# A two-layer conditioned trunk on eight cores: the planner's vector durations and load rate are set to measured values

## The chip, the cores and the metric

The kernel runs on the 8 cores of one Trainium2 chip. Each core takes one of the 8 batch rows and computes it alone, so every core runs the same program on other data. The metric is the device time of the slowest core in microseconds (us), the median of several runs; lower is better. A core has a matrix engine (TensorE, in the rows PE, its weight loads PEld), a vector engine (VectorE, DVE), an activation engine (ScalarE, ACT), a general engine (GpSimd, POOL) and an engine that here only issues transfers (SyncE, SP). Each engine works through its own list of instructions in order, and semaphores tie the lists together.

## What is computed

Batch 8, 4096 positions, width 1024, two layers. Layer 0 mixes positions by a short gated convolution and a gated recurrence, layer 1 by spatial gating; each is followed by a squared-ReLU MLP. Cut to what matters:

```python
for layer in range(2):
    sh1, sc1, g1, sh2, sc2, g2 = ada_modulation(c, ada_w[layer], ada_b[layer])
    h = rmsnorm(x, norm_mix_g[layer]) * (1.0 + sc1) + sh1
    if layer == 0:
        p = einsum('bsd,de->bse', h, w_in0)          # 1024 -> 3584
        y = concat([short_conv_mixer(...), hgrn2_mixer(...)]) @ w_out0
    else:
        z = gelu(einsum('bsd,de->bse', h, w_in1) + b_in1)   # 1024 -> 2048
        y = spatial_gating_mixer(z, ...) @ w_out1
    x = x + g1 * y
    h = rmsnorm(x, norm_ffn_g[layer]) * (1.0 + sc2) + sh2
    hid = square(relu(h @ w_ff1[layer]))             # 1024 -> 4096
    x = x + g2 * (hid @ w_ff2[layer])                # 4096 -> 1024
return rmsnorm(x, final_g)
```

## The kernel before

A core's 4096 positions are 8 tiles of 512. The work goes through six stages, one after the other, each over all 8 tiles: the mixer of layer 0 (phase_m0, 82 to 641 us of the profiled execution), its MLP in two passes (p 0: 562 to 1059, p 1: 1043 to 1462), the mixer of layer 1 (phase_m1, 1438 to 1831), and its MLP in two passes (1803 to 2252, 2237 to 2653). x lies in HBM between the stages; each pass of an MLP holds half of the hidden width, 8 weight slots of 2 MiB, and the slots are refilled as the last tile of the stage before gives them up (L582: 2 MiB of float32 in HBM, which land as 1 MiB of bfloat16). Every stage begins a tile with a norm: squares of the 8 chunks of x on ScalarE (L693 and L696), their sum on GpSimd (L699), one product on TensorE (L701), then L703 and L705 on ScalarE.

A pass with p 0 is ff1 (product groups of 8 matmuls at L750, evicted by ScalarE at L1207 and squared at L1210 or, on VectorE, at L1213) and ff2_plain (L1328, added to x by VectorE at L1340). A pass with p 1 computes its products with 7 instead of 8 half-size products: ff1_halves and ff2. In ff1_halves a tile has 8 columns m, and each goes through three groups of 8 matmuls of 256 columns (0.87 us each) in one PSUM bank, all of them recorded at L1233, with a fourth, shared by two columns:

- first(m): ScalarE copies half of the bank out (L1247), VectorE adds the other half (L1248);
- shared(i): VectorE subtracts it from the two parts (L1269);
- second(m): it writes over the half that L1247 and L1248 have read, so it waits for both; ScalarE evicts it (L1260) and squares it (L1254);
- third(m): it writes over what L1260 has read, so it waits for that; VectorE adds the part (L1278), and ReLU and square follow (L1282 on VectorE for some columns, else L1286 and L1254 on ScalarE).

ff2 does the same with four columns (products at L1371, copies at L1394 and L1396, the shared product's at L1407, additions to x at L1378). Its last part is stage(m, (7, 6)) for m 0 to 3.

No instruction's place is written by hand. Each call of pe, act, dve or dma records an operation with its reads and writes, a key (when it is wanted, in us) and a duration. Graph.schedule then plays the program through with these durations: whenever an engine is free, it takes the available operation with the lowest key, and that becomes the engine's order. A duration is a number for ordering alone; nothing on the chip is delayed by it. VectorE's come from c_dve or stand as numbers; a transfer's is its bytes by a rate:

```python
def c_dve(n, rate=1, ptr=0):
    return 0.155 + n / (960.0 * rate) + 0.06 * ptr
```

With H = 256 and TT = 512, c_dve(H) is 0.422 us, c_dve(TT) 0.688 us, c_dve(H, 1, 1) 0.482 us. What the chip does between two instructions is kept by semaphores whatever the order, so a bad order shows as an engine that waits with its first instruction while a later one is ready.

## Time and profile before

| | us |
|---|---|
| median of 3 runs | 2675.32 (2668.88 to 2678.11) |
| the profiled execution | 2666.36 |
| its span on the slowest core (core 3) | 2664.8 |
| spans of the eight cores | 2655.8 to 2664.8 |
| TensorE, VectorE, ScalarE, GpSimd busy | 2563.7, 1872.8, 1486.2, 853.9 |

The profiled execution is 9.0 us (0.3%) below the median of the runs shown. The views below are of core 3. In a view of the time line each row is a run of instructions of one line: start, length, engine, line, operation, output and input, their number, and in brackets the idle time before it and what ended it. Neighbouring matmuls overlap in the records, so their lengths are compared by the distance of their starts.

### The profile page before, as it was taken

To read this page: it belongs to the slowest core of one execution; us is meant where nothing else is said; L and a number is where in the kernel's file an instruction comes from. 1 tells how busy PE (TensorE), PEld (TensorE's weight loads), DVE (VectorE), ACT (ScalarE), POOL (GpSimd) and SP (SyncE) were. 2 spreads that over 40 slices of the span, in tenths; PEclk is the share of its full clock that TensorE was granted. 3 is DMA by queue.
4 is the path that set the end of the run, shared out by engine and by line. 5 is a ranking of instruction groups with operands and counts; after the bars stand their busy time and mean duration, and the time that the engine had idled before them with its cause. 6 is when DMAs were issued, how large, how long until landed. Compare 5 with 4: busy or idle time off the path is not lost.

```text
span 2664.8 us, 53173 instructions; the slowest of 8 cores (2655.8 to 2664.8 us)
## 1 busy us (share of the span) xinstructions
PE 2563.7 (96%) x18204; PEld 1684.9 (63%) x18204; DVE 1872.8 (70%) x3391; ACT 1486.2 (56%) x2477; POOL 853.9 (32%) x952
## 2 busy tenths in 40 slices
PE   3999999999999999999999999998999999999998
PEld 1444454445666666788887444444766666788887
DVE  3577777777655666887887677776655656787887
ACT  4777777784545553343434676644545553545544
POOL 4555555542533440000002354412434440112111
PEclk9999999999999999999999999999999999999999
DMA  9844444449366348754538666553254336332431
GB/s 191 149 139 112 112 112 109 103 98 199 89 148 147 101 120 149 179 132 131 146 108 171 179 180 190 146 156 110 87 144 134 96 116 152 92 118 80 134 106 64
DMA packets 126426, 348.34 MB, mean 131 GB/s; under 512 B 13904, under 2 KB 16464, under 8 KB 115280
## 3 DMA queue, kind: packets, MB, share of 16 engines
q1 hardware_dynamic: 106464, 265.77, 32.9%
q0 software_dynamic: 19152, 78.65, 18.1%
q8 instruction: 149, 2.44, 0.4%
q14 instruction: 117, 0.96, 0.1%
q10 hardware_dynamic: 544, 0.52, 0.1%
HBM read 301.90 MB, written 117.44 MB: 157 GB/s over the span
## 4 chain that ended last, share of the span: by engine, by line
PE 79%; DMA 7%; POOL 4%; issue 3%; ACT 3%; DVE 3%; SPq 0%; DVEq 0%; ACTq 0%; POOLq 0%
PE ps L750 25%; PE ps L1328 14%; PE ps L1371 14%; PE ps L1233 10%; PE ps L1639 4%; PE ps L1584 3%; PE ps L1018 3%; POOL sb_arena L699 2%; DMA sb_arena<-xs 2%; PE ps L1193 2%; DMA xs<-sb_arena 2%; PE ps L991 2%; DMA sb_arena<-w_in 1%; DMA sb_arena<-x 1%; DMA sb_arena<-w_ff 1%
## 5 line engine op out<-in xcount | busy, mean ns | idle before, releaser
L750 PE MATMUL ps<-sb_arena 128*128 128x512 bf16 x4096 | 923.0, 381 | 6.5 <-DMA sb_arena<-w_in 6.5
L750 PEld LDWEIGHTS ps<-sb_arena 128*128 128x128 bf16 x4096 | 396.2, 98 | 463.8 <-issue 13.7
L699 POOL TENSOR_TENSOR sb_arena<-sb_arena 128x512 f32<-128x512 f32 (+1 forms) x259 | 357.1, 1379 | 795.9 <-ACT sb_arena L696 772.0
L1328 PE MATMUL ps<-sb_arena 128*128 128x256 bf16 x3584 | 402.9, 274 | 5.4 <-DVE sb_arena L1213 5.3
L1371 PE MATMUL ps<-sb_arena 128*128 128x256 bf16 x3584 | 398.6, 273 | 4.7 <-DVE sb_arena L1378 4.7
L1328 PEld LDWEIGHTS ps<-sb_arena 128*128 128x128 bf16 x3584 | 351.7, 98 | 57.3 <-issue 8.1
L1371 PEld LDWEIGHTS ps<-sb_arena 128*128 128x128 bf16 x3584 | 350.4, 98 | 46.8 <-issue 5.7
L1233 PE MATMUL ps<-sb_arena 128*128 128x256 bf16 x3136 | 351.9, 272 | 2.1 <-DVE sb_arena L1248 1.6
L1207 ACT ACTIVATE sb_arena<-ps 128x512 f32<-128x512 f32 x288 | 170.7, 594 | 292.8 <-PE ps L750 211.3
L1233 PEld LDWEIGHTS ps<-sb_arena 128*128 128x128 bf16 x3136 | 304.9, 98 | 43.3 <-issue 8.0
L1340 DVE SCALAR_TENSOR_TENSOR sb_arena<-ps,sb_arena 128x256 f32<-128x256 f32 x640 | 261.1, 474 | 87.3 <-PE ps L1328 86.2
L1311 DVE TENSOR_TENSOR sb_arena<-sb_arena 128x1024 bf16<-128x1024 bf16 x320 | 249.4, 815 | 65.6 <-ACT sb_arena L1210 57.4
L696 ACT ACTIVATE sb_arena<-sb_arena 128x512 f32<-128x512 f32 x273 | 169.1, 624 | 104.3 <-POOL sb_arena L699 40.8
L1213 DVE TENSOR_TENSOR sb_arena<-sb_arena 128x512 bf16<-128x512 f32 x90 | 77.9, 865 | 170.7 <-ACT sb_arena L1207 170.7
L412 ACT ACT_TABLE_LOAD x128 | 164.2, 1283 | 57.6 <-PE ps L750 30.1
L1176 POOL TENSOR_TENSOR sb_arena<-sb_arena 128x512 f32<-128x512 f32 x112 | 138.4, 1275 | 99.0 <-ACT sb_arena L705 98.8
L1179 ACT ACTIVATE sb_arena<-sb_arena 128x512 bf16<-128x512 f32 x128 | 103.8, 813 | 72.7 <-POOL sb_arena L1176 61.9
L1378 DVE SCALAR_TENSOR_TENSOR sb_arena<-ps,sb_arena 128x256 f32<-128x256 f32 x256 | 110.5, 477 | 41.5 <-PE ps L1371 38.4
L1210 ACT ACTIVATE sb_arena<-sb_arena 128x512 bf16<-128x512 f32 x198 | 124.4, 628 | 15.1
L1639 PE MATMUL ps<-sb_arena 128*128 128x512 bf16 x512 | 121.6, 384 | 9.4 <-DVE sb_arena L1632 7.1
L740 DVE SCALAR_TENSOR_TENSOR sb_arena<-ps,sb_arena 128x512 f32<-128x512 f32 x128 | 94.3, 740 | 42.6 <-PE ps L1018 26.8
L1584 PE MATMUL ps<-sb_arena 128*128 128x512 bf16 x512 | 121.7, 382 | 1.8 <-ACT sb_arena L727 1.8
(152 smaller groups left out, 3066.8 us busy)
## 6 DMA issues: line engine op xcount, KB each, us to landing
xs<-sb_arena SPq DMA_DIRECT2D x320, 256.0 KB, 4.5
sb_arena<-xs SPq DMA_DIRECT2D x160, 512.0 KB, 6.5
sb_arena<-w_ff POOLq DMA_DIRECT2D x32, 1024.0 KB, 12.9
sb_arena<-ada_w POOLq DMA_DIRECT2D x72, 256.0 KB, 4.9
sb_arena<-x SPq DMA_DIRECT2D x64, 256.0 KB, 3.9
hs<-sb_arena SPq DMA_DIRECT2D x16, 1024.0 KB, 12.8
sb_arena<-hs SPq DMA_DIRECT2D x16, 1024.0 KB, 5.2
sb_arena<-xs SPq DMA_DIRECT2D x64, 256.0 KB, 4.6
```

Source lines behind the costliest of these rows:

```text
L412: eng.preload_act_table_set(op.table)
L696: act(lambda e, c=c, ap=ap: e.activation(out=tmp[:, c % 2, :], in_=ap, func=AF.Square), b, [tmpb[c % 2]], key, c_act(512))
L699: G.add(adds, lambda e, c=c, to=to: e.tensor_tensor(out=to, in0=dst, in1=tmp[:, c % 2, :], op=ALU.add), [b_dst, tmpb[c % 2]], [b_to], key, ...
L750: parts = [(lambda e, kc=kc: e.matmul(bk(B), w[:, kc, col0:col0 + 128], hT[:, kc, :], start=kc == 0, stop=kc == 7), [wb, hb[kc]], c_mm(512 ...
L1207: act(lambda e, B=B, q=q: e.activation(out=rt[:, q, :], in_=bk(B), func=AF.Relu), [B], rtb[2 * q:2 * q + 2], k, c_act(TT, True))
L1233: parts.append((lambda e, kc=kc, r=r, w=w: e.matmul(bk(B)[:, col:col + H], w[:, kc, (m % 4) * 128:(m % 4) * 128 + 128], r[:, kc, :], start ...
L1311: dve(lambda e, xa=xa, ya=ya, da=da, op=op: e.tensor_tensor(out=da, in0=xa, in1=ya, op=op), xbufs + ybufs, dbufs, k + (8.0 if u == 0 else ...
L1328: parts.append((lambda e, m=m, fc=fc, h=h, r=r: e.matmul(bk(Bm)[:, h * H:(h + 1) * H], w[:, fc, m * 128:(m + 1) * 128], r, start=h == 0 an ...
L1340: dve(lambda e, h=h, x=x, g=g: e.scalar_tensor_tensor(out=x, in0=bk(Bm)[:, h * H:(h + 1) * H], scalar=g, in1=x, op0=ALU.mult, op1=ALU.add) ...
L1371: parts.append((lambda e, fc=fc, r=r: e.matmul(bk(B)[:, col:col + H], w[:, fc, m * 128:(m + 1) * 128], r, start=start and fc == 0, stop=fc ...
L1584: o = pe([(lambda e, kc=kc, g=g, hh=hh, B=B, hT=hT: e.matmul(bk(B), hT[:, kc, g * 128:(g + 1) * 128], win[2 + hh][0][:, kc, :], start=kc == 0,
L1639: pe([(lambda e, kk=kk, c=c, B=B, wv=wv: e.matmul(bk(B), wv[:, kk, (c % 4) * 128:(c % 4) * 128 + 128], ymix[:, kk, :], start=kk == 0, stop ...
```

## The change

Six numbers that VectorE operations are recorded with, and the rate of transfers. No operation is added, removed or given another key; what changes is the play through, and with it the order on each engine.

```diff
@@ Graph.schedule
-                        t = pick.nbytes / 280e3
+                        t = pick.nbytes / 320e3
@@ first (L1248), shared (L1269), ff2's first (L1396) and shared_product (L1407)
-                        0.34)
+                        c_dve(H))
@@ third (L1278)
-                        [B, tb], [zb], k - 20, 0.62)
+                        [B, tb], [zb], k - 20, c_dve(TT))
@@ ff2's add (L1378)
-                        0.38)
+                        c_dve(H, 1, 1))
```

A transfer of 2 MiB is thus planned with 6.55 us in place of 7.49.

Where the orders differ on TensorE: in the first tiles of phase_m0 (60 to 230 us), at the seam of phase_m0 and the MLP (655 to 685), a little in each tile of the first p 0 pass, in each tile of both p 1 passes, and from 1440 to 1550, the seam of the MLP and phase_m1. From 230 to 655 and from 1554 to 2289 it is the same.

Three places in the listing of the orders. In each row: line, operation, output and input, shape, and how many stand together.

ScalarE where tile 0 of the MLP's ff1 ends and tile 1's norm begins, before (L1207 and L1210 are tile 0's evictions, L693 and L696 tile 1's squares):

```order
712 L1210 ACTIVATE sb_arena<-sb_arena 128x2x256
713 L1207 ACTIVATE sb_arena<-ps 128x512
714 L1210 ACTIVATE sb_arena<-sb_arena 128x2x256
715 L1207 ACTIVATE sb_arena<-ps 128x512
716 L693 ACTIVATE sb_arena<-sb_arena 128x512
717 L696 ACTIVATE sb_arena<-sb_arena 128x512 x7
718 L412 ACT_TABLE_LOAD
```

And in the changed kernel:

```order
714 L1207 ACTIVATE sb_arena<-ps 128x512
715 L693 ACTIVATE sb_arena<-sb_arena 128x512
716 L696 ACTIVATE sb_arena<-sb_arena 128x512
717 L1207 ACTIVATE sb_arena<-ps 128x512
718 L1210 ACTIVATE sb_arena<-sb_arena 128x2x256
719 L696 ACTIVATE sb_arena<-sb_arena 128x512 x2
720 L1207 ACTIVATE sb_arena<-ps 128x512
721 L1210 ACTIVATE sb_arena<-sb_arena 128x2x256
722 L696 ACTIVATE sb_arena<-sb_arena 128x512
723 L1207 ACTIVATE sb_arena<-ps 128x512
724 L696 ACTIVATE sb_arena<-sb_arena 128x512 x3
```

The last three evictions of tile 0 stood ahead of all eight squares of tile 1. Now the first of them stands behind two squares, the second behind four and the third behind five.

TensorE where the last tile of the MLP's second pass ends and phase_m1 begins, before (L1371 is ff2, L1584 and L750 are phase_m1's input products, of its two weight pairs):

```order
519 L1371 MATMUL ps<-sb_arena 128x256 x188
520 L1584 MATMUL ps<-sb_arena 128x512 x24
521 L750 MATMUL ps<-sb_arena 128x512 x8
522 L1584 MATMUL ps<-sb_arena 128x512 x32
523 L750 MATMUL ps<-sb_arena 128x512 x8
524 L1584 MATMUL ps<-sb_arena 128x512 x8
525 L750 MATMUL ps<-sb_arena 128x512 x8
526 L701 MATMUL ps<-sb_arena 128x512
```

And in the changed kernel:

```order
527 L1371 MATMUL ps<-sb_arena 128x256 x192
528 L750 MATMUL ps<-sb_arena 128x512 x16
529 L1371 MATMUL ps<-sb_arena 128x256 x32
530 L1584 MATMUL ps<-sb_arena 128x512 x24
531 L750 MATMUL ps<-sb_arena 128x512 x8
532 L1584 MATMUL ps<-sb_arena 128x512 x8
533 L701 MATMUL ps<-sb_arena 128x512
534 L1584 MATMUL ps<-sb_arena 128x512 x8
```

Two product groups of L750 now stand ahead of the last two stages of ff2 (32 matmuls); before, the first of them stood behind these and behind three groups of L1584.

ScalarE in tile 3 of the last pass, from the eviction of second(3) to that of second(5), before (L1247 copies a first, L1260 evicts a second, L703 and L705 are the norm of the final output):

```order
1802 L1260 ACTIVATE sb_arena<-ps 128x512
1803 L705 ACTIVATE sb_arena<-sb_arena 128x512
1804 L1254 ACTIVATE sb_arena<-sb_arena 128x2x256
1805 L1286 ACTIVATE sb_arena<-sb_arena 128x512
1806 L1254 ACTIVATE sb_arena<-sb_arena 128x2x256
1807 L1247 ACTIVATE sb_arena<-ps 128x256
1808 L1254 ACTIVATE sb_arena<-sb_arena 128x2x256
1809 L1247 ACTIVATE sb_arena<-ps 128x256
1810 L1260 ACTIVATE sb_arena<-ps 128x512
1811 L1254 ACTIVATE sb_arena<-sb_arena 128x2x256
1812 L1260 ACTIVATE sb_arena<-ps 128x512
```

And in the changed kernel:

```order
1823 L1254 ACTIVATE sb_arena<-sb_arena 128x2x256 x2
1824 L1286 ACTIVATE sb_arena<-sb_arena 128x512
1825 L1247 ACTIVATE sb_arena<-ps 128x256
1826 L1254 ACTIVATE sb_arena<-sb_arena 128x2x256
1827 L703 ACTIVATE sb_arena<-ps,sb_arena 128x512
1828 L1254 ACTIVATE sb_arena<-sb_arena 128x2x256
1829 L1260 ACTIVATE sb_arena<-ps 128x512
1830 L705 ACTIVATE sb_arena<-sb_arena 128x512
1831 L1247 ACTIVATE sb_arena<-ps 128x256
1832 L1254 ACTIVATE sb_arena<-sb_arena 128x2x256
1833 L1247 ACTIVATE sb_arena<-ps 128x256
1834 L1260 ACTIVATE sb_arena<-ps 128x512
```

The copies of first(4) and first(5) stood one operation apart and now stand five apart, with the norm's L703 and L705 and the eviction of second(4) between them.

TensorE's groups follow. In this tile its order from second(3) on is, before: second 3, third 2, third 3, first 4, first 5, shared 2, second 4, second 5, first 6, third 4, first 7, third 5, second 6, second 7, shared 3, third 6, third 7, with the norm's L701 ahead of second 3. In the changed kernel it is: second 3, third 2, third 3, first 4, L701, second 4, first 5, shared 2, third 4, first 6, second 5, third 5, first 7, second 6, shared 3, second 7, third 6, and the first group of ff2 ahead of third 7. Tiles 2 to 7 of the last pass have this pattern, six in all. All these groups are of one line, so the listing shows only where L701 stands, before and then changed:

```order
773 L1371 MATMUL ps<-sb_arena 128x256 x32
774 L1233 MATMUL ps<-sb_arena 128x256 x80
775 L701 MATMUL ps<-sb_arena 128x512
776 L1233 MATMUL ps<-sb_arena 128x256 x136
777 L1371 MATMUL ps<-sb_arena 128x256 x192
```

```order
789 L1233 MATMUL ps<-sb_arena 128x256 x48
790 L1371 MATMUL ps<-sb_arena 128x256 x32
791 L1233 MATMUL ps<-sb_arena 128x256 x72
792 L701 MATMUL ps<-sb_arena 128x512
793 L1233 MATMUL ps<-sb_arena 128x256 x96
```

L701 moved four groups of 8 matmuls nearer to the end of the tile's ff1, and the last stages of the tile before (L1371, 32 matmuls), which stood behind one group of the new tile, stand behind six.

## Rows read from the trace of the kernel before

**Rows 1.** The page, busy time of each engine, share of the span, instructions.

```profile
PE 2563.7 (96%) x18204; PEld 1684.9 (63%) x18204; DVE 1872.8 (70%) x3391; ACT 1486.2 (56%) x2477; POOL 853.9 (32%) x952
```

**Rows 2.** Busy time per stretch: us, PE, PEld, DVE, ACT, POOL, clock, DMA, GB/s.

```profile
2313.10:2611.20 298.10, 296.73 (x2697) 263.33 (x2697) 239.68 (x488) 151.76 (x301) 55.05 (x42) 1.00 0.34 107
```

**Rows 3.** Groups by line and form: count, busy us, mean ns, idle before, releasers.

```profile
L1378 DVE SCALAR_TENSOR_TENSOR sb_arena<-ps,sb_arena 128x256 f32<-128x256 f32 x256 | 110.5, 477 | 41.5 <-PE ps L1371 38.4 <-PE ps L1472 2.3
L1278 DVE TENSOR_TENSOR sb_arena<-ps,sb_arena 128x512 f32<-128x512 f32 x112 | 77.1, 689 | 40.7 <-PE ps L1233 39.1 <-DVE sb_arena L1278 0.2
L1248 DVE TENSOR_TENSOR sb_arena<-ps,sb_arena 128x256 f32<-128x256 f32 x112 | 46.5, 419 | 16.5 <-ACT sb_arena L1247 16.0 <-issue 0.3
L1407 DVE TENSOR_TENSOR sb_arena<-ps,sb_arena 128x256 f32<-128x256 f32 x64 | 25.0, 416 | 5.2 <-PE ps L1371 3.8 <-PE ps L1472 1.0 <-DVE sb_arena L1165 0.2
```

**Rows 4.** The five loads of w_in issued from 42.6 to 44.7 us.

```profile
DMA to landing us min/median/max: 21.7/32.9/44.5
```

**Rows 5.** Two loads of w_in, issued at 1423.0 and 1423.5 us.

```profile
DMA to landing us min/median/max: 10.0/13.8/17.7
```

**Rows 6.** The load of w_in issued at 1435.6 us, three after the one at 1423.5.

```profile
DMA to landing us min/median/max: 29.9/29.9/29.9
```

**Rows 7.** Time line of TensorE, then of ScalarE, start of phase_m0.

```profile
64.07 0.56 PE L895 MATMUL ps<-sb_arena 128*128 128x32 bf16 x15 [2.37 <-POOL sb_arena L868]
...
111.34 1.15 ACT L696 ACTIVATE sb_arena<-sb_arena 128x512 f32<-128x512 f32 x2 [6.28 <-DMA sb_arena<-x]
```

**Rows 8.** Time line of ScalarE, seam of phase_m0 and the MLP.

```profile
652.66 0.63 ACT L1210 ACTIVATE sb_arena<-sb_arena 128x512 bf16<-128x512 f32 x1
654.07 0.60 ACT L1207 ACTIVATE sb_arena<-ps 128x512 f32<-128x512 f32 x1 [0.78 <-DVE sb_arena L1213]
657.23 0.63 ACT L693 ACTIVATE sb_arena<-sb_arena 128x512 f32<-128x512 f32 x1 [2.56 <-DMA sb_arena<-xs]
657.76 0.62 ACT L696 ACTIVATE sb_arena<-sb_arena 128x512 f32<-128x512 f32 x1
...
661.48 0.63 ACT L696 ACTIVATE sb_arena<-sb_arena 128x512 f32<-128x512 f32 x1 [1.34 <-POOL sb_arena L699]
```

**Rows 9.** Time line of TensorE, same seam.

```profile
653.52 14.13 PE L1328 MATMUL ps<-sb_arena 128*128 128x256 bf16 x128
671.92 0.58 PE L701 MATMUL ps<-sb_arena 128*128 128x512 bf16 x1 [4.26 <-POOL sb_arena L699]
672.29 12.75 PE L1328 MATMUL ps<-sb_arena 128*128 128x256 bf16 x96
```

**Rows 10.** Time line of TensorE, seam of the MLP and phase_m1.

```profile
1458.45 3.65 PE L1371 MATMUL ps<-sb_arena 128*128 128x256 bf16 x32 [2.03 <-DVE sb_arena L1378]
...
1467.12 1.89 PE L750 MATMUL ps<-sb_arena 128*128 128x512 bf16 x8
...
1482.94 0.38 PE L701 MATMUL ps<-sb_arena 128*128 128x512 bf16 x1 [1.85 <-POOL sb_arena L699]
...
1493.39 0.38 PE L1584 MATMUL ps<-sb_arena 128*128 128x512 bf16 x1 [0.57 <-ACT sb_arena L727]
...
1495.18 0.38 PE L1584 MATMUL ps<-sb_arena 128*128 128x512 bf16 x1 [0.81 <-ACT sb_arena L727]
...
1497.03 3.19 PE L1584 MATMUL ps<-sb_arena 128*128 128x512 bf16 x9
```

**Rows 11.** Time line of TensorE, tile 3 of the last pass.

```profile
2412.03 0.38 PE L701 MATMUL ps<-sb_arena 128*128 128x512 bf16 x1
2412.25 15.13 PE L1233 MATMUL ps<-sb_arena 128*128 128x256 bf16 x136
```

**Rows 12.** Groups by line and form, ScalarE's copies and evictions of ff1_halves.

```profile
L1260 ACT ACTIVATE sb_arena<-ps 128x512 f32<-128x512 f32 x112 | 66.2, 591 | 61.8 <-PE ps L1233 60.8
L1247 ACT ACTIVATE sb_arena<-ps 128x256 f32<-128x256 f32 x112 | 42.3, 377 | 102.5 <-PE ps L1233 102.4
```

6 lines of the change are left out of this document (3 added, 3 removed).

## The prediction, made before the changed kernel was run

> **What bounds the kernel now.** The page comes first: TensorE is busy 2563.7 of 2664.8 us [rows 1], and no other engine passes 70%. A shorter operation on VectorE would buy nothing; what the change can move is the time in which TensorE waits. So the second view is the time line of TensorE at the places where its order or that of a neighbour differs, and the third the time line of the neighbour that it waits for. In the last pass the steady state has little left: six tiles in 298.1 us [rows 2], 49.7 each. A 256-column matmul costs 0.109 us (128 in 14.13, less the tail of the last [rows 9]), so the 448 of a tile and one L701 are 49.1, and about 0.6 us of each tile is waiting. The larger waits are at the seams: 4.3 us ahead of L701 at 671.9 and some 2.2 us more because the 96 matmuls behind it take 12.75 where 10.5 would do [rows 9], and 2.0, 1.9 and 1.8 us (four pieces, two of them shown) between 1456 and 1496 [rows 10].
>
> **Are the new numbers right?** The durations are: VectorE's 0.34 were 0.419 and 0.416 in the trace, 0.62 was 0.689, 0.38 was 0.477 [rows 3], and the new ones are 0.422, 0.688 and 0.482. The rate is right in one place: of the first five loads the last landed 44.5 us after its issue at 44.7 and the first 21.7 after 42.6 [rows 4], four loads of 2 MiB in 24.9 us, 6.2 each, or 337e3 bytes/us. In another it isn't: a load issued at 1423.5 landed at 1441.2 [rows 5], the third behind it, issued at 1435.6, at 1465.5 [rows 6]: 24.3 us for three, 259e3. There x is being stored and loaded as well. The planner's model puts a share of such traffic on top, but its base is now 14% faster. So where weights gate a product, the plan counts on them earlier than they come.
>
> A correct number is no gain by itself. The orders differ, and each place has to be costed. Operations before and after are the same in number, so the cost of the edit is the sum of waits made less waits removed.
>
> **Start of phase_m0 (60 to 230): 0 us.** Products whose weights are there move ahead of a group that waited 2.4 us for GpSimd [rows 7]. But ScalarE then stands at a square of x's third tile until 111.3, and waits 6.3 us for that load [rows 7]; TensorE is fed from behind it. What is gained at 64 is waited for at 109. Behind 120 neighbouring groups change places, with nothing waited there before. Bounds: -2.4 if the load came to matter no more, +1.
>
> **Seam of phase_m0 and the MLP (650 to 690): +6 us.** The product at 653.5 starts 0.2 us after the square of 652.7 ends at 653.3 [rows 8, 9]. That square belongs to the second of tile 0's last three evictions, which now stand behind squares of tile 1. ScalarE's first square of tile 1 waits for x until 657.2 [rows 8]. With the durations of the rows: squares to 658.4, first eviction and its square to 659.6, two more squares, of which the second waits for GpSimd until 661.5, to 662.1, second eviction and square to 663.3. The product starts at 663.5, 10.0 later. Five groups of 1.76 us follow (16 matmuls each), 672.3, and the clock falls as after the 4.3 us of before, 2.2: 674.5. L701 now stands here and its sum is there (before at 671.8), then three groups: 679.8, where the old order was at 672.3 and still had its 2.2 to pay. Difference 7.5 - 2.2 = 5.3, and a few tenths for the third eviction (L1207 at 654.1, now at 664), on which a VectorE square and the next product hang: 6. Bounds: 3, if that x load lands as much earlier as SyncE has room, 9, if the longer idle time keeps the clock low twice as long. The next tile's input hangs on L701, which comes 2.6 later, and is covered by the 5.3.
>
> **First p 1 pass (1090 to 1434): +1 us.** The pairs second and third of a column come to stand one group apart in two more places per tile. Where they do so before, as at third 3 in the tile of [rows 11], a wait of some 0.1 us is left; seven tiles give 1. Bounds 0 and 3.
>
> **Seam of the MLP and phase_m1 (1456 to 1500): +4.6 us.** TensorE ended the stage of column 1 at 1456.4 (2.03 us of idle time before 1458.45 [rows 10]). Its next group is now L750, whose weights are those of [rows 6]: 1465.5. It stands at the head of its list for 9.2 us, and the two stages, ready at 1458.4, and three L1584 groups queue behind it. Before, these were done first, and L750 at 1467.1 waited for nothing [rows 10]. So 9.2 in place of 2.0: +7.2. The clock then costs 2.2, by [rows 9]. Against it, what was waited for later has 7 us more to come: L701's 1.9, L727's 1.8, and the slow matmuls behind them (nine in 3.19 where 2.1 would do) 1.1 [rows 10]. 7.2 + 2.2 - 4.8 = 4.6. Bounds: 1, if the clock holds and the load lands 1.5 earlier, and 9.4, if the norm chain slips by as much as TensorE does (its squares share ScalarE with evictions that are late).
> By the Trainium skill (DMA: Bandwidth & Descriptors, section "Issuing engines are not separate DMA queues"), transfers started by different engines interleave on the same 16 engines, which speaks against planning one fixed rate for weights; the two rates above agree with it. Were the three loads to come at the new rate, 19.7 us, they would land at 1460.9, and this term would be 0.
>
> **Last pass, tiles 2 to 7: +8.4 us.** Two pairs have lost their distance. (a) second(4) now follows first(4) with only L701 (0.2 us) between; there were two groups before. It needs the copy (0.377 [rows 12]) and the add (0.419 [rows 3]), and three handovers of 0.2 as at 653.3: 1.4, less 0.2: 1.2. L701 itself waits in that time, since the stages that finish x are five groups later and its sum with them. (b) third(5) follows second(5) at once, where a group stood between them before. It needs the eviction, 0.591 [rows 12], and the handovers, less the overlap of one matmul's tail: 0.9. Before, the same 17 groups took 15.13 us for 14.8 of work [rows 11], with next to nothing waited. Against 2.1 stands the 0.6 us per tile of before, most of it ahead of second 2 and L701, which the new places remove. 1.5 less 0.1 for what stays: 1.4, six times. Bounds: 3 (0.5 a tile, if only (b) counts) and 13 (2.1, nothing removed).
>
> **Sum**: 0 + 6 + 1 + 4.6 + 8.4 = 20 us. On the profiled execution 2666.4 + 20 = 2686; on the median of the runs, which lies 9 us above it, **2695**. With all lower bounds (-2.4 + 3 + 0 + 1 + 3) the sum is 5, with all upper bounds (1 + 9 + 3 + 9.4 + 13) 35.
>
> **The rivals.**
> *No measurable change (2675 to 2683).* The waits are made but slack takes them in. For it: TensorE is not held by any one chain for long; half the waits at the seams of before are for a next tile's norm, which has hardly any room. If the seams give 2 each and the last pass 0.5 a tile, the sum is 7: 2682. Against it: in the last pass nothing follows in which a wait could be made good, since TensorE's own work sets the pace there.
> *Faster (2665).* Right durations let the planner see VectorE's queue as it is, so that TensorE's head of line is what really comes first. The 0.6 us of six tiles (3.6), the 4.8 us after 1480 and the 2.4 us at 64 go: -10.8. It decides at two arrivals: the weight load would have to land by 1456.4 rather than 1465.5, and x by 650 rather than 657.2; and (a) and (b) would have to be shorter than their own copies. Nothing in the rows does that, but orders interact over 2000 groups and five places were followed.
> *Slower by more (2710).* Operations that are late hold what is behind them on ScalarE and VectorE: at both seams the upper bounds hold, and in the last pass copies queue behind L703 and L705: 35 us.
> *The change does nothing.* Excluded in this form: the listed orders differ.
>
> **Chances.** My forecast (2684 to 2704) 0.55; slower by more 0.18; no measurable change 0.18; faster by over 0.3% 0.09. A difference of under 0.3%, 8 us, is about what a measurement of this kernel can't tell from none. Slower than 2683.3 is thus 0.73, within 0.18, faster 0.09. The range reaches from 2672, which takes in most of the unchanged cases, to 2710.
>
> **What would show it.** In the changed kernel's trace: TensorE idle for 9 to 10 us ahead of L1328 near 654, and for some 9 us ahead of L750 near 1456, released by the load; a clock below 1 in both stretches; no wait for L701 near 672; tiles of the last pass at 51 us rather than 49.7, with waits for L1248 and L1260 that were not listed before; phase_m1 from 1554 on and the first pass of layer 1 as long as they were. I am wrong if the period of the last pass stays at 49.7, for then (a) and (b) are covered, and on the other side if a place that I took for unchanged, the p 0 passes above all, grows.

## The result: 2725.8 us, 2.0% slower than before

| | before | changed |
|---|---|---|
| median (range), 4 runs each | 2672.1 (2667.8 to 2678.1) | 2725.8 (2720.1 to 2733.8) |
| the profiled execution, slowest core | 2664.8 | 2726.0 |
| the profiled execution, fastest core | 2655.8 | 2684.1 |

The ratio is 1.0198, 95% interval 1.0176 to 1.022, or 53.7 us. The direction was forecast, the size was not: 20 us, and a range that ended at 2710. Measured again later (run e5), the same kernel was at 1.0133 (1.0108 to 1.0159), 36 us. Ratios and intervals leave out executions in which one die took over 1% longer than the other at a lower granted clock.

In each of the first four runs one pair of cores, not always the same, had a granted clock of 0.975 to 0.979 where the others had 0.984 to 0.991, and spans 6 to 29 us longer than the median of the others; in the runs of e5 that were compared no pair did. In the profiled execution it was cores 0 and 1, and they lost it early: 163.0 and 165.4 us in the first stretch of the table below against 148.3 to 151.3 on the other six, and 3.5 more in the second. So some 36 to 41 us are what the order costs (the ratio of e5 and the medians of the table), and the rest came with that pair.

The page of the changed kernel, busy time of each engine, against [rows 1]:

```profile
PE 2580.0 (95%) x18008; PEld 1692.8 (62%) x18204; DVE 1889.5 (69%) x3391; ACT 1495.2 (55%) x2481; POOL 857.3 (31%) x952
```

The work is the same; ScalarE has four instructions more, all of them table loads. (The 196 matmuls fewer on TensorE are records that the trace of core 0 lacks; the weight loads are all 18204 there.) The page is of core 0, one of the pair with the low clock. The rest is read on core 3, as before, whose clock was 0.990. Some of what TensorE waited for there over the whole span (us in total, times, longest), before and then changed:

```profile
PE ps L701 <- POOL sb_arena L699: 28.6, 6, 20.2
PE ps L1328 <- DVE sb_arena L1213: 5.3, 6, 2.0
PE ps L1233 <- DVE sb_arena L1248: 1.6, 2, 1.4
```

```profile
PE ps L1328 <- ACT sb_arena L1210: 8.5, 2, 5.8
PE ps L1233 <- ACT sb_arena L1260: 8.0, 8, 2.2
PE ps L1621 <- DVE sb_arena L1608: 7.4, 5, 5.6
PE ps L1233 <- DVE sb_arena L1248: 5.6, 7, 2.6
```

(20.2 us of L701's are the wait for the first data at the start; in the changed kernel another instruction stands first there and waits 20.1.) L1210 and L1260 are evictions' chains, as forecast. L1621 is new: the spatial mixing product of phase_m1, which needs VectorE's L1608, which needs two small operations of ScalarE (L1602, L1604, on 128x4).

To see where the time went I marked first products on TensorE in every trace. Medians over the eight cores of one execution each, us:

| stretch | before | changed | e5, again | e1 rate | e2 durations | e3 add | e7 change, x late | e9 before, x late | e11 weights' rate |
|---|---|---|---|---|---|---|---|---|---|
| first L750 to phase_m0 tile 2 | 147.7 | 150.1 | 150.1 | 149.2 | 147.2 | 147.0 | 145.3 | 148.3 | 147.1 |
| rest of phase_m0 | 415.3 | 416.2 | 416.1 | 416.1 | 415.5 | 415.6 | 414.8 | 415.5 | 414.3 |
| seam to the MLP (its first two tiles) | 124.8 | 129.1 | 129.2 | 129.0 | 124.8 | 125.0 | 132.4 | 132.2 | 129.3 |
| rest of the p 0 pass | 303.6 | 304.2 | 303.1 | 303.4 | 304.9 | 304.5 | 300.8 | 305.4 | 303.5 |
| first p 1 pass, tiles 0 to 6 | 364.3 | 362.4 | 363.5 | 362.7 | 362.2 | 362.0 | 361.1 | 360.1 | 365.1 |
| seam to phase_m1 (tile 7 to its tile 2) | 132.8 | 148.5 | 145.9 | 143.5 | 149.2 | 144.5 | 145.5 | 134.7 | 134.2 |
| rest of phase_m1 | 290.0 | 289.4 | 290.4 | 289.9 | 296.0 | 292.1 | 291.5 | 290.4 | 289.6 |
| p 0 pass of layer 1 | 407.8 | 412.7 | 412.6 | 404.9 | 406.9 | 407.2 | 405.9 | 406.0 | 404.4 |
| last pass | 416.5 | 430.8 | 432.1 | 416.2 | 431.8 | 423.9 | 432.6 | 416.2 | 416.2 |

The changed kernel's column adds up to 40.6 us more than before's: 15.7 at the seam to phase_m1, 14.3 in the last pass, 4.9 in the first pass of layer 1, 4.3 at the first seam, 2.4 at the start. The columns from e5 on come from other sets of runs than the column of before, and their sums differ from what the measured ratios say by up to 11 us (e7: 27 by the column, 16 by the ratio). In the kernel before the cores lie 0.3 us apart in the last pass and up to 6 us apart at the start and at the seams, so a difference of 2 us there says little.

The first seam, TensorE and then ScalarE of the changed kernel, against [rows 8, 9] (start, length, engine, line, what, and in brackets the idle time before and its cause):

```profile
659.44 0.37 PE L1328 MATMUL ps<-sb_arena 128*128 128x256 bf16 x1 [5.79 <-ACT sb_arena L1210]
662.53 8.48 PE L1328 MATMUL ps<-sb_arena 128*128 128x256 bf16 x61 [2.72 <-ACT sb_arena L1210]
...
673.44 0.38 PE L701 MATMUL ps<-sb_arena 128*128 128x512 bf16 x1
```

```profile
656.94 0.63 ACT L693 ACTIVATE sb_arena<-sb_arena 128x512 f32<-128x512 f32 x1 [5.54 <-DMA sb_arena<-xs]
...
658.00 0.58 ACT L1207 ACTIVATE sb_arena<-ps 128x512 f32<-128x512 f32 x1
658.67 0.63 ACT L1210 ACTIVATE sb_arena<-sb_arena 128x512 bf16<-128x512 f32 x1
...
661.76 0.63 ACT L1210 ACTIVATE sb_arena<-sb_arena 128x512 bf16<-128x512 f32 x1
```

The square L693 waits for x until 656.9, and the two evictions behind it end at 659.3 and 662.4, each 0.14 us ahead of the product that needs it. The prediction had 659.6, 663.3 and 663.5. L701 waits for nothing.

The seam to phase_m1, TensorE, against [rows 10]:

```profile
1426.13 6.19 PE L1233 MATMUL ps<-sb_arena 128*128 128x256 bf16 x40 [2.16 <-ACT sb_arena L1260]
1434.91 3.91 PE L1233 MATMUL ps<-sb_arena 128*128 128x256 bf16 x32 [2.59 <-DVE sb_arena L1248]
...
1462.20 3.61 PE L750 MATMUL ps<-sb_arena 128*128 128x512 bf16 x16 [1.87 <-DMA sb_arena<-w_in]
...
1504.44 0.27 PE L1621 MATMUL ps<-sb_arena 128*128 128x128 bf16 x1 [5.57 <-DVE sb_arena L1608]
```

ScalarE ahead of the first two of these:

```profile
1423.83 0.63 ACT L696 ACTIVATE sb_arena<-sb_arena 128x512 f32<-128x512 f32 x1 [2.22 <-DMA sb_arena<-xs]
1424.37 0.61 ACT L1254 ACTIVATE sb_arena<-sb_arena 128x512 bf16<-128x512 f32 x1
...
1425.41 1.06 ACT L1260 ACTIVATE sb_arena<-ps 128x512 f32<-128x512 f32 x2
```

VectorE:

```profile
1425.08 6.43 DVE L1311 TENSOR_TENSOR sb_arena<-sb_arena 128x1024 bf16<-128x1024 bf16 x4 [2.15 <-ACT sb_arena L1254]
...
1434.35 0.41 DVE L1248 TENSOR_TENSOR sb_arena<-ps,sb_arena 128x256 f32<-128x256 f32 x1
```

At 1423.8 a square of phase_m1's first norm has waited 2.2 us for its part of x, and the evictions L1260 behind it free TensorE at 1426.1. The second wait, 2.59 us for L1248, reaches back to the same square by way of VectorE: L1254 stands behind the square, VectorE's sums L1311 have waited 2.15 us for it, and four of them (6.43 us) stand ahead of L1248. (The kernel before waits for L1248 at this place too, 1.36 us.) None of this is in the prediction, which looked at this seam from 1456 on.

The last pass, TensorE, one tile, against [rows 11]:

```profile
2379.90 5.40 PE L1233 MATMUL ps<-sb_arena 128*128 128x256 bf16 x48 [0.84 <-ACT sb_arena L1260]
...
2424.61 0.38 PE L701 MATMUL ps<-sb_arena 128*128 128x512 bf16 x1 [0.63 <-POOL sb_arena L699]
2425.49 5.40 PE L1233 MATMUL ps<-sb_arena 128*128 128x256 bf16 x48 [0.51 <-DVE sb_arena L1248]
2431.73 5.40 PE L1233 MATMUL ps<-sb_arena 128*128 128x256 bf16 x48 [0.84 <-ACT sb_arena L1260]
```

From third(5) to third(5), 2379.90 to 2431.73, is 51.8 us, 49.7 before [rows 2].

### The profile page after: what moved, and what is told of

Same layout as the page of the kernel before. It is cut to its first block, busy times and chain, and to the rows that moved or that the text cites. A ratio compares the mean times of both kernels' runs of the same rounds, so it can differ in the third digit from the quotient of the medians.

```text
span 2726.0 us, 53013 instructions; the slowest of 8 cores (2684.1 to 2726.0 us)
## 1 busy us (share of the span) xinstructions
PE 2580.0 (95%) x18008; PEld 1692.8 (62%) x18204; DVE 1889.5 (69%) x3391; ACT 1495.2 (55%) x2481; POOL 857.3 (31%) x952
## 4 chain that ended last, share of the span: by engine, by line
PE 80%; DMA 9%; DVE 3%; issue 3%; ACT 3%; POOL 1%; DVEq 0%; ACTq 0%; SPq 0%; POOLq 0%
PE ps L750 25%; PE ps L1328 13%; PE ps L1371 13%; PE ps L1233 12%; PE ps L1639 4%; DMA xs<-sb_arena 4%; PE ps L1584 4%; PE ps L1018 3%; DMA sb_arena<-w_in 2%; DMA sb_arena<-xs 2%; PE ps L991 2%; PE ps L1193 1%; DVE sb_arena L1213 1%; PE ps L1621 0%; DMA sb_arena<-hs 0%
## 5 line engine op out<-in xcount | busy, mean ns | idle before, releaser
L750 PE MATMUL ps<-sb_arena 128*128 128x512 bf16 x3974 | 927.2, 386 | 16.8 <-DMA sb_arena<-w_in 9.8
L750 PEld LDWEIGHTS ps<-sb_arena 128*128 128x128 bf16 x4096 | 400.4, 99 | 478.6 <-issue 70.4
L699 POOL TENSOR_TENSOR sb_arena<-sb_arena 128x512 f32<-128x512 f32 (+1 forms) x259 | 358.6, 1384 | 845.0 <-ACT sb_arena L696 795.2
L1371 PE MATMUL ps<-sb_arena 128*128 128x256 bf16 x3584 | 400.1, 273 | 5.3 <-DVE sb_arena L1378 3.4
L1371 PEld LDWEIGHTS ps<-sb_arena 128*128 128x128 bf16 x3584 | 350.2, 98 | 48.0 <-issue 6.8
L1207 ACT ACTIVATE sb_arena<-ps 128x512 f32<-128x512 f32 x288 | 169.5, 592 | 294.2 <-PE ps L750 206.6
L1311 DVE TENSOR_TENSOR sb_arena<-sb_arena 128x1024 bf16<-128x1024 bf16 x320 | 253.0, 826 | 92.6 <-ACT sb_arena L1210 81.3
L696 ACT ACTIVATE sb_arena<-sb_arena 128x512 f32<-128x512 f32 x273 | 167.9, 623 | 83.9 <-DMA sb_arena<-xs 30.4
L1179 ACT ACTIVATE sb_arena<-sb_arena 128x512 bf16<-128x512 f32 x128 | 103.7, 813 | 73.6 <-POOL sb_arena L1176 62.2
L1378 DVE SCALAR_TENSOR_TENSOR sb_arena<-ps,sb_arena 128x256 f32<-128x256 f32 x256 | 111.6, 477 | 39.0 <-PE ps L1371 34.6
L1210 ACT ACTIVATE sb_arena<-sb_arena 128x512 bf16<-128x512 f32 x198 | 124.3, 628 | 16.2 <-ACT sb_arena L1207 1.1
L1639 PE MATMUL ps<-sb_arena 128*128 128x512 bf16 x500 | 121.2, 387 | 10.2 <-DVE sb_arena L1632 8.1
L1254 ACT ACTIVATE sb_arena<-sb_arena 128x512 bf16<-128x512 f32 x196 | 118.7, 625 | 7.3
```

The costliest lines, as they stand in the source:

```text
L696: act(lambda e, c=c, ap=ap: e.activation(out=tmp[:, c % 2, :], in_=ap, func=AF.Square), b, [tmpb[c % 2]], key, c_act(512))
L699: G.add(adds, lambda e, c=c, to=to: e.tensor_tensor(out=to, in0=dst, in1=tmp[:, c % 2, :], op=ALU.add), [b_dst, tmpb[c % 2]], [b_to], key, ...
L750: parts = [(lambda e, kc=kc: e.matmul(bk(B), w[:, kc, col0:col0 + 128], hT[:, kc, :], start=kc == 0, stop=kc == 7), [wb, hb[kc]], c_mm(512 ...
L1207: act(lambda e, B=B, q=q: e.activation(out=rt[:, q, :], in_=bk(B), func=AF.Relu), [B], rtb[2 * q:2 * q + 2], k, c_act(TT, True))
L1311: dve(lambda e, xa=xa, ya=ya, da=da, op=op: e.tensor_tensor(out=da, in0=xa, in1=ya, op=op), xbufs + ybufs, dbufs, k + (8.0 if u == 0 else ...
L1371: parts.append((lambda e, fc=fc, r=r: e.matmul(bk(B)[:, col:col + H], w[:, fc, m * 128:(m + 1) * 128], r, start=start and fc == 0, stop=fc ...
```

## The experiments

Three theories stood at the start. **A**: each moved operation costs where it now stands, and the parts add up. **B**: neither the rate nor the durations alone do harm, only the seam order that both together make. **C** came up with the traces of the changed kernel: the plan counts on x earlier than SyncE's loads bring it, so ScalarE has squares of the next norm at the head of its list, waiting, with evictions behind them. In all stretches quoted the medians over the cores are meant.

### The parts of the change: e1 to e5

**e1**, the rate alone:

```diff
-                        t = pick.nbytes / 280e3
+                        t = pick.nbytes / 320e3
```

> Only the planned transfer rate is changed (280e3 to 320e3 bytes/us), VectorE's numbers stay as before. Theory A (each part of the change costs where it moves operations, and the parts add up): the start of phase_m0 costs 5 us, the seam at 650 us 3 to 6, the first pass of layer 1 5 to 10 on some cores, because ScalarE's first squares of a tile stand ahead of an x load that hasn't landed, and one pair of cores loses 10 more at a lower granted clock between 60 and 240 us. That is +22 to +32 us, 2694 to 2704, with the last pass at 49.7 us a tile. Theory B (the seam with phase_m1 is what costs, and only both halves of the change together put L750 ahead of the last stages): under +12 us.

Measured: 1.0034 (1.0013 to 1.0056). That is 9 us, which fits B (under 12) and not A (22 to 32). The first seam takes its whole loss from the rate (129.0), the seam to phase_m1 most of it (143.5 against 132.8), the last pass none.

**e2**, the six durations alone (the other lines of the diff):

> Only the six durations are changed, the rate stays 280e3. Theory A: +14 us in the last pass (51.8 us a tile where before had 49.7), 3 less in the first p 1 pass, up to 8 at the seam with phase_m1: +14 to +20 us, 2686 to 2692, no pair of cores with a low clock at the start, and e1 and e2 together make up the 53.7 us. Theory B: +14, and e1 and e2 together make up less than 35 us.

Measured: 1.0134 (1.0082 to 1.0186), from two of its four runs: 36 us, which neither theory had. The last pass has all of its loss (431.8), the seam to phase_m1 as much as the whole change has (149.2).

**e3**, only L1378's number:

```diff
-                        0.38)
+                        c_dve(H, 1, 1))
```

> Only the duration of ff2's additions to x (L1378) is changed, 0.38 to 0.482. Theory A: this number is what moves the groups of the last pass, so nearly all of its cost is here: +10 to +15 us, 2682 to 2687, the last pass at 51 us a tile or more. Rival: the ff1_halves numbers (0.34 and 0.62) matter more, since the waits are at their operations: under +4 us here.

Measured: 1.0039 (1.0025 to 1.0054), 10 us; half of the last pass's loss (423.9), where A had nearly all of it, and most of the loss at the seam to phase_m1 (144.5).

**e4**, the other five numbers:

> The other five durations are changed, the additions keep 0.38, the rate stays 280e3. Theory A: the last pass keeps its old places up to third 7 and 49.7 us a tile; the first p 1 pass gains 2 to 3; the seam costs up to 5: within 4 us of before. Rival: +10 or more, as the evictions and adds of ff1_halves are planned longer and so reordered.

Measured: 1.0022 (0.9995 to 1.005), which can't be told from none.

**e5**, the changed kernel again, in a later set of runs:

> The changed kernel once more, beside the others of this set. In its first four runs one pair of cores (0 and 1, or 2 and 3, or 4 and 5) had a granted clock of 0.975 to 0.979 and spans some 20 us longer than the rest; no run of the kernel before, or of the rate alone, had that. If the order makes it (dense products between 60 and 240 us), it is here again: 2720 to 2734 us. If it came with the chip or the hour, the slowest core is at 2700 to 2712.

Measured: 1.0133 (1.0108 to 1.0159). The stretches are those of the first profile within 3 us. Rate and durations apart give 9 and 36 us, together 36. B falls, since each alone costs 10 us or more at the seam to phase_m1, and A holds only roughly. The durations don't add up either (10 and 6 us apart, 36 together). A list order is no sum of edits.

### The last pass: e6, e12, e14, e15

**e6**, the changed kernel with the old six numbers for operations of layer 1 (one of the six places):

```diff
-                        c_dve(H, 1, 1))
+                        (0.38 if l else c_dve(H, 1, 1)))
```

> The whole change, but the last pass keeps its old durations (0.34, 0.62, 0.38). Theory A: the last pass goes back to 49.7 us a tile and 416.5 us in all, and nothing else moves: 14 us less than e5. Rival (the last pass is slow because the cores arrive there late and uneven): under 5 us less.

Measured: 1.0089 (1.0067 to 1.0111), 12 us less than e5; the last pass 416.5, as before.

**e12**, the changed kernel's order with short copies, additions and evictions in layer 1, so that most of its hidden values are left out (the copy alone, cut):

```diff
-  act(... out=t, in_=bk(B)[:, 0:H], func=AF.Copy)
+  act(... out=t[:, 0:64], in_=bk(B)[:, 0:64], func=AF.Copy)
```

> The changed kernel, its order kept to the last instruction, but in layer 1 the copies of L1247 and the additions of L1248 work on 64 of 256 columns and the evictions of L1260 on 128 of 512 (the rest of the hidden values isn't computed). This shortens the three operations that second and third wait for by about 0.15, 0.2 and 0.35 us. If the last pass is longer because TensorE waits for these chains with nothing else at the head of its list (prediction (a) and (b)), five tiles come from 259.1 to 253 to 256 us, and TensorE's waits for L1260 and L1248 fall below half. If it is VectorE's or ScalarE's place elsewhere, the stages of ff2 or the norm, the tiles stay within 1 us of 259.1. All else as the changed kernel: 1.013 less 3 to 6 us.

**e14**, the changed kernel's order with GpSimd's sums of the final norm on 64 of 512 columns, which leaves out the rest of the sum, and **e15**, both:

> The changed kernel, its order kept to the last instruction, but GpSimd's seven additions of the final norm (L699 in the last pass) work on 64 of 512 columns, so that L701 has its sum much sooner (the norm is wrong for the other columns). In the changed kernel TensorE stood 0.8 us ahead of L701 and 0.7 more ahead of the second group behind it, in each tile. If L701's sum is what is late there and second(4)'s own chain is covered by it, 5 tiles of the last pass come from 259.1 us to 255 to 257. If second(4) waits 1.2 by its own chain (the prediction's (a)), the wait only changes its name from L699 to L1248 and the tiles gain 0.3 each at most: 257.5 to 259.

> Both shortenings of the last pass in the changed kernel's order: GpSimd's sums as in the one above and the copies, additions and evictions as in the run with short copies (255.6 us for five tiles). If the two chains end at the same product, neither alone helps much and both together do: 251 to 253. If they are separate, the gains add up. If something else holds TensorE there (the stages of ff2 or bank limits), it stays above 255.

Five tiles of the last pass: 259.1 us in the changed kernel, 255.6 with short copies, 258.1 with short sums, 254.5 with both (before: 248.3). The kernel with short copies was at 1.0096 (1.0063 to 1.0129). Of what TensorE waits for in that stretch (core 3, 2375 to 2630 us), first the changed kernel of e5, then e14:

```profile
PE ps L1233 <- ACT sb_arena L1260: 4.2, 5, 0.8
PE ps L701 <- POOL sb_arena L699: 3.3, 5, 0.9
PE ps L1233 <- DVE sb_arena L1248: 2.5, 5, 0.5
```

```profile
PE ps L1233 <- DVE sb_arena L1248: 5.7, 5, 1.1
PE ps L1233 <- ACT sb_arena L1260: 4.2, 5, 0.8
```

With the sums short the wait for L699 (0.7 a tile) only changes its name: 0.5 + 0.7 for L1248 and L699 become 1.1 for L1248. That is the prediction's (a), forecast at 1.2. With L1247, L1248 and L1260 at 0.22, 0.22 and 0.28 us instead of 0.38, 0.42 and 0.59 as well (e15), (a) is 0.9 and (b) 0.5, where the prediction's way of adding up, two or three handovers of 0.2 us between engines and the operations, gives 0.8 and 0.6. So both chains are what the prediction said, and what the short operations leave of them is mostly handovers. The two gains add up (3.5, 1.0 and together 4.6), so two separate chains are shortened, not one. Short copies alone (e12) brought the waits for L1260 and L1248 down to 2.6 and 1.5, six tenths of what they were, not below half. Of the 10.8 us that the changed order costs in these tiles the runs took away 4.6; that the other 6.2 are mostly the same two waits is read from the trace (0.9 + 0.5 in each of five tiles) and not shown by taking them away.

### SyncE's loads of x: e7 to e11

**e7**, the changed kernel planned with SyncE's transfers landing 4 us later (in the plan alone):

```diff
-                            pick.fin = dma_free
+                            pick.fin = dma_free + 4.0
```

> The whole change, and the planner adds 4 us to the landing of each transfer that SyncE issues (x in and out, h), so that it puts ScalarE's squares of the next tile later. Theory C (what the rate costs is squares that stand ahead of evictions while x is on its way): ScalarE's waits for x at the seams and in the first pass of layer 1 go, and 10 to 20 us with them; the last pass keeps its 14 us. Rival: the weights' rate makes those costs: no gain.

Measured: 1.006 (1.0041 to 1.0079), 20 us less than e5, more than half of the loss. The p 0 pass of layer 1, where TensorE's order is the same in all three kernels, is back at 405.9. ScalarE's waits for x on core 0 from its tile 2 to its end, before, e5 and e7 (busy, mean ns, idle before, its cause):

```profile
L693 ACT ACTIVATE sb_arena<-sb_arena 128x512 f32<-128x512 f32 x5 | 3.1, 629 | 6.9 <-DMA sb_arena<-xs 6.9
```

```profile
L693 ACT ACTIVATE sb_arena<-sb_arena 128x512 f32<-128x512 f32 x5 | 3.1, 630 | 11.5 <-DMA sb_arena<-xs 11.5
```

```profile
L693 ACT ACTIVATE sb_arena<-sb_arena 128x512 f32<-128x512 f32 x5 | 3.1, 622 | 0.0
```

And TensorE's for the squared values behind them, in the same order:

```profile
PE ps L1328 <- DVE sb_arena L1213: 3.2, 4, 1.3
```

```profile
PE ps L1328 <- DVE sb_arena L1213: 5.0, 5, 1.4
```

```profile
PE ps L1328 <- DVE sb_arena L1213: 0.9, 4, 0.2
```

That stretch took 304.6 to 308.5 us on the eight cores before, 309.0 to 315.6 in e5, and 304.5 or 304.6 on every core in e7. The spread between the cores goes together with the wait for x. At the seam to phase_m1, though, e7 gained nothing (145.5 against 145.9): L1608's wait fell to 1.7 to 2.4 us, but others came (4.7 or 4.8 for L1378 on every core, up to 4.1 for L1626).

**e8**, before with the same lateness; **e9**, the same only past 620 us of the plan; **e10**, as e9 with 2 us:

```diff
-                            pick.fin = dma_free
+                            pick.fin = dma_free + (4.0 if now > 620.0 else 0.0)
```

> The kernel before with the same 4 us added to the landing of SyncE's transfers. Theory C: the kernel before loses little to this, so -5 to 0 us: 53 to 54 us at the seam with phase_m1, 303.5 in the first pass of layer 1 on all cores. Rival: an added latency is one more reshuffle, and costs as others do: +5 to +15.

> The kernel before, planned with SyncE's transfers landing 4 us later, but only past 620 us of the plan, so that phase_m0 keeps its order. Theory C (squares that stand ahead of evictions while x is on its way cost time): the gains of the run with 4 us everywhere stay (first tiles of the MLP 119.9 in place of 124.8 us, tiles 2 to 7 of its second pass 246.8 in place of 249.9, first pass of layer 1 304.8 in place of 306.6) and phase_m0's loss of 15.4 goes: 5 to 10 us faster than before, ratio 0.996 to 0.998. Theory A (each part costs where it moves operations): the orders are only other orders, and the ratio is 1.000 within 0.002. The seam of the MLP and phase_m1, 53.6 before, is at 57.5 by the run with 4 us everywhere in either case.

> As the one above with 2 us in place of 4, past 620 us of the plan. Theory C: half the room, so ScalarE's squares still stand ahead of evictions at the first seam (124.8 us as before), while the seam of the MLP and phase_m1 comes to 54 to 58 and its wait for squares is the same or shorter; ratio 0.998 to 1.000. Theory A: 1.000.

Measured: e8 1.0012 (0.9994 to 1.003), e9 0.999 (0.998 to 1.0), e10 1.0021 (0.9995 to 1.0047). In e8 the passes gained and phase_m0 lost 15.4. In e9 phase_m0 was as before, the first p 1 pass 4.2 and the first of layer 1 1.8 better, but the first seam, whose order was now another, 7.4 worse. C had 5 to 10 us less than before for e9, and that didn't come. No kernel of this study is measurably faster than before. C names a true cause, but a truer number for x is no better a recipe than truer numbers for VectorE.

**e11**, the new rate only for GpSimd's transfers (weights):

```diff
-                        t = pick.nbytes / 280e3
+                        t = pick.nbytes / (320e3 if e == "pool" else 280e3)
```

> The kernel before with the rate of 320e3 for GpSimd's transfers (weights and stores that GpSimd issues) and 280e3 for SyncE's. If what costs is that weights are counted on too early (the prediction's reason), the seam of the MLP and phase_m1 is at 62.8 us as with the whole rate and the kernel is 9 us slower (1.0034). If it is SyncE's x loads (theory C), that seam stays at 53.6, its order being the old one, and what is left is the start of phase_m0 (+6 and -3) and the seam of phase_m0 and the MLP, whose ScalarE order is the new one (+4): +7 at most, 1.0015 to 1.003.

Measured: 1.0012 (0.9983 to 1.0041), the seam to phase_m1 134.2. So of e1's loss there the weights have 1.4 of 10.7; the rest needs SyncE's share of the rate. At the seam to phase_m1 a load of x takes 10.4 us from issue to landing (changed kernel, core 3, 1395 to 1470 us), where the plan has 1.6 for its 512 KB by the new rate and a fixed 2.6:

```profile
sb_arena<-xs SPq DMA_DIRECT2D x8, 512.0 KB, 10.4
```

At the first seam it is the other way round: the weights' rate alone brings all of the loss (129.3).

### TensorE's wait for L1608: e13, e16, e17

**e13**, the changed kernel; the first square of tile 2 in phase_m1 is planned after tile 0's L1604 (cut):

```diff
-                        c_act(512))
+                        c_act(512), after=rsop[:1] if late == 4.0 and len(rsop) == 2 else ())
```

> The changed kernel with one more ordering constraint in the plan: in phase_m1 ScalarE's first square of tile 2 (L693) may not stand ahead of tile 0's L1602 and L1604, two operations on 128x4. TensorE's order stays that of the changed kernel. In the changed kernel, run again, this square stood at the head of ScalarE's list for 4.8 us on core 3, waiting for x, with L1602 behind it, and TensorE waited 7.6 us for L1608, which needs L1604. Theory C (ScalarE's squares, planned for when x was thought to land, hold what stands behind them): TensorE's wait for L1608 falls from 4 to 9 us to 1 to 3 on every core, the time from the first product of the last tile of the MLP to the first of phase_m1's tile 2 (146 us in the changed kernel run again, 132.3 before) to 140 to 142, and the kernel gains 4 to 6. Rival: the norm of tile 2 has no room either, TensorE waits for its L701 or the products behind it instead, and the sum stays at 146, the kernel within 2 us.

Measured: 1.0129 (1.0097 to 1.0161); the wait for L1608 was 5.0 to 11.0 on the eight cores, no less (3.2 to 9.4 in e5). The reason is in the trace, ScalarE on core 3: the second square took the place of the first.

```profile
1505.31 0.63 ACT L696 ACTIVATE sb_arena<-sb_arena 128x512 f32<-128x512 f32 x1 [4.72 <-DMA sb_arena<-xs]
...
1507.26 0.30 ACT L1602 ACTIVATE sb_arena<-sb_arena 128x4 f32<-128x4 f32 x1
```

The run thus said nothing on the cause. **e16** holds all eight squares, **e17** is its control on the same chip (cut):

```diff
-                    b, [tmpb[c % 2]], key, c_act(512))
+                    b, [tmpb[c % 2]], key, c_act(512), after=rsop[:1] if late == 4.0 and len(rsop) == 2 else ())
```

> The changed kernel with the constraint of the run before made whole: in phase_m1 none of ScalarE's eight squares of tile 2 may stand ahead of tile 0's L1602 and L1604. (In the run before only the first was held; the second took its place and waited 4.7 us for x with L1602 behind it, so that run didn't test the cause.) TensorE's order stays that of the changed kernel, apart from a few groups near 1590 of the plan. Theory C: L1602 is ready at about 1501 on core 3 and no longer waits for x until 1505; TensorE's wait for L1608 falls from 3 to 9 us to 1 to 4 on every core, the time from the first product of the last tile of the MLP to phase_m1's tile 2 (146 us in the changed kernel run again) to 141 to 143, and the kernel is 3 to 6 us faster than the changed kernel of the same call. Rival: the norm of tile 2, whose x lands at 1505 in either case, has no room, TensorE waits as long for its L701 or what hangs on it, and nothing is gained.

> The changed kernel once more, unchanged, as the control of the run beside it. By its two earlier measurements 1.013 to 1.020 of the kernel before; 146 us over the seam, TensorE waiting 3 to 9 us for L1608.

On that chip cores 0 to 3 had a granted clock of 0.967 to 0.975 in both profiles, so no ratio is given, and cores 4 to 7, at 0.985 to 0.989, are compared. In e16 on core 4 the square waits 4.4 us for x all the same, but the two small operations stand ahead of it:

```profile
1504.33 0.30 ACT L1602 ACTIVATE sb_arena<-sb_arena 128x4 f32<-128x4 f32 x1
1504.72 0.20 ACT L1604 ACTIVATE sb_arena<-sb_arena 128x4 f32<-128x4 f32 x1
1509.36 0.63 ACT L693 ACTIVATE sb_arena<-sb_arena 128x512 f32<-128x512 f32 x1 [4.44 <-DMA sb_arena<-xs]
```

TensorE's waits for L1608, first e16 on core 4, then e17 on core 7, where x landed 6.8 us after ScalarE was ready for its square:

```profile
PE ps L1621 <- DVE sb_arena L1608: 2.4, 5, 0.5
```

```profile
PE ps L1621 <- DVE sb_arena L1608: 11.0, 4, 9.6
```

On the four cores it is 2.4, 2.7, 5.4, 4.5 in e16 and 4.7, 5.2, 11.4, 11.0 in e17, so about half of the wait goes; on cores 0 to 3 it is 3.5 to 4.6 and 2.6 to 4.7, and nothing goes. What it is worth is less clear: on cores 4 to 7 the seam took 143.9 to 149.1 in e16 and 145.7 to 154.2 in e17, but 143.8 to 150.1 in e5. It is 0 to 4 us, and the seam didn't come to the 141 to 143 expected.

Not all of this wait has to do with x. In the first profile of the changed kernel the square stands on four cores (2, 4, 5 and 7) at the head of ScalarE's list without a wait, and TensorE waits 4.2 to 4.7 us for L1608 there; on the four where the square waits 2.2 to 5.5 us for x it is 7.4 to 9.6. ScalarE and TensorE on core 4:

```profile
1507.60 0.63 ACT L693 ACTIVATE sb_arena<-sb_arena 128x512 f32<-128x512 f32 x1
...
1509.62 0.30 ACT L1602 ACTIVATE sb_arena<-sb_arena 128x4 f32<-128x4 f32 x1
```

```profile
PE ps L1621 <- DVE sb_arena L1608: 4.2, 4, 2.7
```

In the kernel before, on core 3, the square of tile 2 waited 4.2 us for x as well, at 1499.9, but L1602 had long been done:

```profile
1485.54 0.29 ACT L1602 ACTIVATE sb_arena<-sb_arena 128x4 f32<-128x4 f32 x1
```

In the changed kernel it runs at 1500.1 on that core. L1602 needs the statistics of all eight L1584 groups of tile 0. Before, these stood close together on TensorE and the last began at 1477.5; in the changed order L750 groups stand between them and the last begins at 1488.4, 10.9 later. That this is what leaves L1608 late without any wait for x fits the times, and no run here took it away alone.

## Why the prediction was right in sign and wrong in size

The point of departure held: VectorE's old numbers were wrong and the new ones right (0.476, 0.690, 0.420 and 0.419 us in the changed kernel's last pass for L1378, L1278, L1248 and L1407), no engine but TensorE bounds the kernel, and nothing but its waits moved.

**Start, 0 forecast, 2.4 measured.** That is above the bound of 1 but not clear of the spread of the cores (145.9 to 151.9 before, 148.3 to 151.3 on the six cores without the low clock now). Which wait it is was not followed.

**First seam, 6 forecast, 4.3 measured** (6.7 on core 3). The mechanism and its times are those of the trace within 1.1 us: TensorE waits 8.5 us (5.79 and 2.72) for the evictions where 10 were forecast in one piece, and L701's 4.3 is gone.

**First p 1 pass, 1 forecast, -0.8 to -1.9 measured.** The 1 us can't be seen.

**Seam to phase_m1, 4.6 forecast, 13.1 to 15.7 measured: the step that failed most.** What was costed did happen: L750 waits for w_in ahead of the last two stages. It was mis-sized, 1.9 to 6.9 us on the eight cores of the first profile instead of 9.2: on core 3 TensorE came there at 1460.3, not 1456.4, and the load had landed at 1462.2, not 1465.5. By the Trainium skill (DMA: Bandwidth & Descriptors, section "Issuing engines are not separate DMA queues") transfers started by different engines interleave on the same 16, which speaks against one fixed rate for weights. That this one wait spreads over 5 us from core to core agrees. What the prediction put at nothing is larger. Two waits in tile 7, ahead of 1456, are 2.2 and 2.6 us on core 3 (1.4 before), and both reach back to a square that waits for x at the head of ScalarE's list. The wait for L1608 is 4.2 to 9.6 us. Of this some 3 to 5 are there only where such a square waits for x; 4.2 to 4.7 are there without it. What causes that part is open; L1602, which stands ahead of it, runs at 1500.1 on core 3, 14.6 us later than before. A square at the head of the list is the mechanism that the prediction worked out for the first seam. It was applied to one of the places where squares had moved, not to all. And the changed order was only followed up to 1500.

**The p 0 passes, 0 forecast.** In the median that of layer 0 was (0.6). That of layer 1 grew by 4.8 to 4.9: TensorE's order is the same there, and from this the prediction took it as unchanged. ScalarE's squares had moved up by one place among the evictions, with x landing behind them (e7). How much it costs hangs on the landing: 404.2 to 419.7 us on the eight cores, 405.8 to 409.6 before. The text named this as the way to be wrong.

**Last pass, 8.4 forecast, 14.3 measured (15.6 in e5).** (a) and (b) are in the trace at 1.1 to 1.4 and 0.8 us, 2.0 a tile together. The failed step is the set-off. Of the 2.1 forecast, 0.6 a tile were said to go with the old waits, and nothing went: the tile is 2.2 longer, not 1.4. The working has a slip there too. If 0.1 of the 0.6 stays, the tile is 1.6 longer, not 1.4, and the sum 21 rather than 20. Six tiles of 2.2 make 13, the upper bound given. The first two tiles add 0.9 (66.1 and 46.3 before, 62.6 and 50.7 now).

**One core, and luck.** The sum was made on core 3. That core's span grew by 19.3 us (2664.8 to 2684.1), nearly the 20 forecast, but by luck: 6.7 at the first seam, 12.2 at the seam to phase_m1 and 14.2 in the last pass are 33, and 14 came back in stretches from which nothing was expected, 5.6 of it in the rest of the first p 0 pass (308.7 to 303.1). On the median core no such gain set it off: 2702.4 against 2660.4, 42 us.

**The clock of a pair.** No term of the sum stood for it. The metric is the slowest of eight cores, and in each of the first four runs that was one of a pair with a lower granted clock, 6 to 29 us behind the median of the other six. At e5's ratio the time would be 2708 (an estimate, 2672.1 by 1.0133), still inside the range, though nearer to the rival of 2710 than to the forecast. So the order, mis-sized as above, brings the time to the end of the range, and the pair takes it past that end.

## What to carry to other kernels

A list scheduler's order is tuned to its numbers, also to the wrong ones: replacing single numbers by measured ones (six durations, the rate, or 4 us more for x) gave ratios from 0.999 to 1.013 and no gain that could be told from none, so each such edit is to be measured as a new order. When an order changes, check every in-order engine and not only the bound one: an engine with the same order can still wait longer for a neighbour that now has an operation that needs a transfer one place earlier. Where an operation waits for a transfer, price what stands behind it on its engine, at every place where that pattern occurs and on the core where the transfer lands last.

## What the hardware showed that I had not expected

The clock of a pair of cores. In the first profile of the changed kernel, cores 0 and 1 ran phase_m0's start at a granted clock well below the others'. Stretch, us, busy PE, PEld, DVE, ACT, POOL, clock, DMA share and GB/s, on core 0 and then on core 3:

```profile
60.00:240.00 180.00, 173.90 (x984) 82.22 (x1004) 109.99 (x172) 131.55 (x204) 89.67 (x134) 0.81 0.54 118
```

```profile
60.00:240.00 180.00, 171.19 (x1127) 85.11 (x1128) 122.19 (x191) 141.51 (x223) 96.07 (x138) 0.97 0.61 136
```

It was another pair in the next run and no pair in e5. Other kernels have it as well: in one run of the kernel before beside e9 cores 6 and 7 were at 0.981 and the others at 0.992 or 0.993, in one of e10 cores 4 and 5 at 0.982 and 0.979, and on the chip of e13 cores 4 to 7 were at 0.974 to 0.984 in the kernel before. What sets it is open; that the change does is not shown.

ScalarE's table loads: the order of phase_m1's first tiles decides how often ScalarE swaps between the functions of the norm and those of GELU (128 table loads in the whole kernel before, 132 now). From 1483.5 to 1491 core 3 in e13, as in e5, loads a table four times at 1.28 us, with one operation between:

```profile
1483.46 1.28 ACT L412 ACT_TABLE_LOAD   x1 [1.24 <-PE ps L701]
1484.75 0.69 ACT L703 ACTIVATE sb_arena<-ps,sb_arena 128x512 f32<-128x512 f32 x1
1485.46 1.28 ACT L412 ACT_TABLE_LOAD   x1
1486.75 0.63 ACT L1594 ACTIVATE sb_arena<-sb_arena 128x512 f32<-128x512 f32 x1
1487.40 1.28 ACT L412 ACT_TABLE_LOAD   x1
1488.69 0.63 ACT L705 ACTIVATE sb_arena<-sb_arena 128x512 f32<-128x512 f32 x1
```

In the kernel before L705 starts 0.8 us after L703 there, here 3.9. How much of the seam's loss this has was not tried.
